# Differential attention on one core: the softmax bias is computed on VectorE instead of ScalarE

## The reference, cut to what matters

```python
def _diff_attend(q, k, v, lam):
    s = jnp.einsum('bhcqd,bhckd->bhcqk', q, k, preferred_element_type=jnp.float32) * (A_DQK ** -0.5)
    p = jax.nn.softmax(s, axis=-1)
    w = p[:, :, 0] - lam * p[:, :, 1]
    return jnp.einsum('bhqk,bhkd->bhqd', w.astype(v.dtype), v)
```

## Time and profile before

| | |
|---|---|
| three executions | 3625.79, 3628.02, 3628.82 us |
| profiled execution | 3625.79 us, span of the trace 3623.9 us |
| busy in the span | PE 3177.8 us (88%), DVE 1710.7 us (47%), ACT 1091.6 us (30%), POOL 301.6 us (8%) |
| costliest lines | PE L562 (the GEMM) 2133.4 + 1405.4 us; in attention PE L657 123.2 us, DVE L1454 194.7 us, ACT L1081 177.6 us |

### The profile page before, as it was taken

How to read it: one execution, slowest core, us unless ns; L and a number is a source line. 1 busy time by engine, 2 the same in 40 slices (tenths; PEclk the granted TensorE clock), 3 DMA queues, 4 the chain that set the end, 5 groups by cost and what they waited for, 6 DMA issues and landing times.

```text
span 3623.9 us, 44488 instructions
## 1 busy us (share of the span) xinstructions
PE 3177.8 (88%) x17262; PEld 1811.7 (50%) x17262; DVE 1710.7 (47%) x2202; ACT 1091.6 (30%) x1730; POOL 301.6 (8%) x208
## 2 busy tenths in 40 slices
PE   6799679778889999999999479679888899999997
PEld 6344554466444665555545234454665344444443
DVE  1794755676356210222225596655674463122235
ACT  2311213566344111111112411213664442111122
POOL 2400010000121000000002240010000210000001
PEclk8999769697999999999999699769898999999998
DMA  5110010111112321111112111011221232111113
GB/s 186 44 41 24 6 37 18 47 52 46 59 56 96 116 87 64 35 37 45 41 47 70 46 41 41 6 37 35 70 69 58 70 105 87 52 49 50 52 52 105
DMA packets 59449, 206.84 MB, mean 57 GB/s; under 512 B 7360, under 2 KB 8384, under 8 KB 59328
## 3 DMA queue, kind: packets, MB, share of 16 engines
q1 hardware_dynamic: 58176, 199.89, 16.5%
q10 hardware_dynamic: 1152, 5.24, 0.4%
HBM read 200.91 MB, written 4.19 MB: 57 GB/s over the span
## 4 chain that ended last, share of the span: by engine, by line
PE 55%; issue 24%; DVE 13%; ACT 5%; POOL 1%; DMA 1%; SPq 0%; POOLq 0%; DVEq 0%; ACTq 0%
PE PS L562 49%; DVE R L1597 4%; DVE wlo L1355 2%; ACT X L1050 1%; ACT R L1048 1%; PE PS L759 1%; DVE R L1433 1%; PE PS L620 1%; ACT whi L1003 1%; DVE R L1420 1%; POOL st L1960 1%; PE PS L815 1%; DVE R L1719 1%; DVE X L1693 0%; POOL X L1891 0%
## 5 line engine op out<-in xcount | busy, mean ns | idle before, releaser
L562 PE MATMUL PS<-R,whi 128*128 128x512 f16 (+1 forms) x7808 | 2133.4, 361 | 119.2 <-DVE wlo L1355 49.0
L562 PE MATMUL PS<-R,wlo 128*128 128x512 f16 (+1 forms) x3904 | 1405.4, 360 | 0.0
L562 PEld LDWEIGHTS PS<-R,whi 128*128 128x128 f16 x7808 | 766.3, 99 | 901.5 <-issue 70.6
L562 PEld LDWEIGHTS PS<-R,wlo 128*128 128x128 f16 x3904 | 385.3, 99 | 382.9 <-issue 19.3
L1355 DVE SCALAR_TENSOR_TENSOR wlo<-stage,whi 128x1024 f16<-128x1024 f32 (+1 forms) x260 | 332.0, 1277 | 512.0 <-ACT whi L1003 495.5
L1003 ACT ACTIVATE whi<-stage 128x1024 f16<-128x1024 f32 (+1 forms) x260 | 268.7, 1033 | 184.3 <-PE PS L562 135.0
L1891 POOL TENSOR_TENSOR X<-X 128x512 f32<-128x512 f32 (+2 forms) x105 | 154.4, 1473 | 1757.4 <-ACT X L1286 1613.6
L1454 DVE TENSOR_REDUCE tiny<-PS 128x1 f32<-128x1280 f32 (+1 forms) x144 | 194.7, 1370 | 96.1 <-PE PS L639 94.3
L1597 DVE SCALAR_TENSOR_TENSOR R<-X,small,R 128x1024 f32<-128x1024 f32 (+1 forms) x180 | 219.2, 1267 | 1.8
L1831 DVE SCALAR_TENSOR_TENSOR X<-X,PS 128x512 f32<-128x512 f32 (+3 forms) x60 | 62.0, 1033 | 303.2 <-PE PS L562 303.2
L1826 DVE SCALAR_TENSOR_TENSOR X<-X,PS 128x512 f32<-128x512 f32 (+3 forms) x60 | 62.1, 1035 | 297.2 <-ACT X L1303 297.2
(11 more groups left out here) (186 smaller groups left out, 2421.2 us busy)
## 6 DMA issues: line engine op xcount, KB each, us to landing
stage<-in_w_gu SPq DMA_DIRECT2D x120, 512.0 KB, 3.5
X<-in_w_ada SPq DMA_DIRECT2D x60, 512.0 KB, 3.4
stage<-in_w_down SPq DMA_DIRECT2D x48, 512.0 KB, 3.4
stage<-in_w_in SPq DMA_DIRECT2D x44, 512.0 KB, 3.4
stage<-in_w_out SPq DMA_DIRECT2D x32, 512.0 KB, 3.5
T<-in_w_ada SPq DMA_DIRECT2D x20, 512.0 KB, 3.5
R<-in_w_ada SPq DMA_DIRECT2D x16, 512.0 KB, 10.3
stage<-in_w_down SPq DMA_DIRECT2D x16, 384.0 KB, 3.0
```

Source lines behind the costliest of these rows:

```text
L562: last = mm(slot(j, t0, t1)[:, c0 - t0:c1 - t0], w[:, j, k, :], row, start=(k == 0 and q == 0), stop=(k == K - 1 and q == 2))
```

## The change

The bias is computed by VectorE, right behind each row maximum, by one `tensor_scalar` on 128x1 values, and ScalarE's two bias instructions go. The maximum is linked to the new instruction through `dve_own`. The semaphore between VectorE and ScalarE, `maxed`, becomes `nbias` and is raised by the new instruction. A new wait holds the new instruction until ScalarE has read the bias of two heads earlier from the same place. ScalarE's chain of own links in attention goes, VectorE's counts 8 more links per tile.

```diff
                 def exps(r, h, c):
                     n = 4 * r + h
-                    act.wait_ge(s("maxed"), 2 * n + (c + 1))
-                    if c:
-                        own.link(A(nbias[:, h % 2, c:c + 1], smax[:, h % 2, c:c + 1], ACT.Copy, scale=-SCORE))
-                    else:
-                        own.link(A(nbias[:, h % 2, c:c + 1], smax[:, h % 2, c:c + 1], ACT.Identity, scale=-SCORE,
-                                   bias=lamv[:, 12 + l:13 + l]))
+                    act.wait_ge(s("nbias"), 2 * n + (c + 1))
                     if not (isinstance(r, int) and n < 2):
 
                         act.wait_ge(s("w"), n - 1)
...
-                per = 2 * HA
                 tile(0, first=True)
                 with act.Fori(1, nt) as r:
-                    own.enter(r - 1, per)
                     tile(r)
-                own.leave(nt - 1, per)
...
                 def maxima(r, h, c):
                     n = 4 * r + h
                     dve.wait_ge(s("scores"), 2 * n + (c + 1))
-                    RED(smax[:, h % 2, c:c + 1], slot(c)[:, 0:keys], AX.X, ALU.max).then_inc(s("maxed"), 1)
+                    own.link(RED(smax[:, h % 2, c:c + 1], slot(c)[:, 0:keys], AX.X, ALU.max))
+                    if not (isinstance(r, int) and n < 2):
+                        dve.wait_ge(s("exps"), 2 * n + (c - 3))
+
+                    TS(nbias[:, h % 2, c:c + 1], smax[:, h % 2, c:c + 1], -SCORE, lamv[:, 12 + l:13 + l] if c == 0 else None,
+                       ALU.mult, ALU.add if c == 0 else ALU.bypass).then_inc(s("nbias"), 1)
...
-                per = 8 + 1 + 2
+                per = 8 + 8 + 1 + 2
```

More of the change, by code:

```diff
@@ L255, in build @@
             for run in (("c", "l") if l < LAYERS - 1 else ("l",)):
-                for n in "scores maxed exps w wt_ps wt pv pv_out".split():
+                for n in "scores nbias exps w wt_ps wt pv pv_out".split():
                     S[f"{n}_{run}{l}"] = sem(f"{n}_{run}_{l}")
```

## The result

The changed kernel took 3644.43 us in the median of 20 executions (3627.69 to 3684.58), the kernel before 3628.06 us beside it (3614.65 to 3637.36). The ratio is 1.0054, with a 95% interval of 1.0031 to 1.0077: slower by about half a per cent, where 0.26% less was forecast. The ratio leaves out the three slowest of them (over 3683 us, more than 1.5% above the fastest), the medians don't. The profiled execution took 3634.09 us, with a span of 3632.3 us; it is one of the quicker ones, so its profile shows less of the loss than the median has.

The account below looks back on a forecast made before the run. The prediction took a loop through several engines as the bound; 6.6 + 2.1 + 1.4 - 0.7 = 9.4 us saved gave 3618.6 us against the median, with 8 in 10 between 3609 and 3629 us.

Parts of the forecast that it names:

- The loop of a head, 0.33 us by the bias of map 0: Latent runs: map 0's exponential starts 0.33 us earlier in 20 heads, all passed on, 6.6 us gained.
- The loop of the context run: Context run: map 1's bias lies on the loop of 2.89 us; some 6 turns x 0.23 = 1.4 us gained.
- the 9.4 us of the sum: Whole kernel: total forecast saving, 6.6 + 2.1 + 1.4 - 0.7 us.
- Map 1's path to the exponential, +0.05 us: Heads 2 of 14 tiles: from maximum's end to exponential 0.05 us longer through VectorE, 0.7 us lost.
- `combine` 0.4 us later and hidden: Head 2: VectorE's extra work delays `combine` by 0.3 to 0.6 us, taken as 0.4, hidden by TensorE's wait for `out_lo`.
- the 0.15 us counted as gained in head 3: Head 3 of 14 tiles: 0.15 of map 0's 0.33 us reaches the modulation products, 2.1 us gained.
- its bad side: Latent runs: long stretches at 1.2 GHz become more; two more cost 12 us, 3631 us; chance 0.08.
- The price of a long stretch, 6.2 us: Latent tiles: one with 24 us at the lower clock takes 37.2 us where most take about 31.
- VectorE becomes the bound: Heads 2 and 3: `combine` late by more than 0.55 us delays TensorE; 14 us slower, 3642 us; chance 0.06.
- Optimizing Scalar/DVE Operations: VectorE against ScalarE: if VectorE is saturated, offloading to ScalarE may make sense; by it the change would be slower.

Follow-up runs that it names:

- map 1 alone: Against the kernel before, VectorE computes only the bias of map 1, ScalarE keeps that of map 0: ratio 1.0055, 3643.32 us.
- map 0 alone: Against the kernel before, VectorE computes only the bias of map 0, ScalarE keeps that of map 1: ratio 0.9948, 3605.76 us.
- The exchange: In head 2 VectorE takes map 1's maximum before `out_sum`: kernel before with it 0.9946, changed kernel with it 0.9969, both against the kernel before.
- the moved group: Layer 0's third group of modulation products moved from head 3 to head 2: before 1.0026, changed 0.9960, only map 0's bias on VectorE 0.9907.
- the added work: Layer 0's third group of modulation products computed also in head 2, first result overwritten: changed kernel 0.9973, only map 0's bias on VectorE 0.9894.
- ScalarE's two kept: Changed kernel, but ScalarE keeps its two bias instructions and writes results nobody reads: ratio 1.0086 to the kernel before, 3656.05 us.
- map 0 and the exchange: Only map 0's bias on VectorE, and map 1's maximum taken before `out_sum` in head 2: ratio 1.0005 to the kernel before, 3623.07 us.

## Why the prediction was wrong

Its own steps, in their order:

- *The loop of a head, 0.33 us by the bias of map 0: right.* 6.66 us a head at full clock, and the wait of 0.48 us shrank to 0.16. The loop of the context run is right as well (2.65 us). But this part alone (map 0) makes the kernel 0.52% faster, some 19 us, twice the 9.4 us of the sum, and the surplus is clock. In layer 1 of the changed kernel the quick tiles went from 30.3 to 28.3 us. Of that 0.32 and 0.40 us, in two heads, are the loop; 1.34 us goes with a stretch of 3.4 us at 1.2 GHz behind head 3. Each quick tile had one of at least that length before (transposes in 1.54 us instead of 0.88, values in 2.10 instead of 1.31); most tiles of layer 1 no longer have it.
- *Map 1's path to the exponential, +0.05 us: right* (+0.04).
- *`combine` 0.4 us later and hidden: mis-sized.* It was 0.6 us, the upper end of the range. TensorE's wait for it rose by 0.56 us, and of the 0.15 us counted as gained in head 3 about 0.06 us is left (from the scores of head 3 to the modulation products 2.78 us pass, before 2.84). By these terms alone the kernel would still be faster.
- *The step that failed: the clock had no term in the sum, and its bad side ("They could also come at other places and be more: two more long stretches cost 12 us") had a chance of 0.08.* The stretches at the lower clock are the largest term, with either sign. In the profiled execution layer 0's six tiles from 720.94 to 938.32 us took 36.2 us on average instead of 31.9; that is 26 us lost, while layer 1 gained 15.4 us. The loop was to save 9.4 us in all. In that run before, one stretch of 24 us stood among ones of 7 us or less; after, there are one of 37 us, two of 24, two of 14 and one of 10. In the median execution the balance is worse: 16 us slower, at a clock of 0.905.
- *The price of a long stretch, 6.2 us: too low.* It was taken against a tile that had a short stretch itself. A tile with 24 us at 1.2 GHz takes 37.7 us and one with 14 us 33.7 to 33.8, instead of 28.3 with none: about 0.4 us lost for each microsecond at that clock, 9.4 us for a long stretch.
- *The rival "VectorE becomes the bound": its place and its point (0.55 us) were passed, but its mechanism isn't what cost the time.* TensorE's longer wait costs little itself, as the quick tiles of layer 1 show, which have it too. The rule of the Trainium skill, "Perfetto Trace Analysis", section "Optimizing Scalar/DVE Operations", spoke against the change. It came out right in its sign for map 1 and not for map 0, and VectorE was not saturated in either. The rule of the Trainium skill, "VectorE: DVE Perf Modes", section "Rules for kernel authors", that the number of instructions counts and not the semaphores, agrees with the times of the two pairs with map 0, where leaving out the wait changed nothing. It does not with the changed kernel: a met wait with its register instruction was 0.09 us of gap each time, and without it the ratio was 0.9974 instead of 1.0054.

What is shown: the loss comes with map 1's part (map 1 alone, map 0 alone), and it goes with more time at the lower clock, in the profile and over all executions. TensorE's idle time in heads 2 and 3 of layer 0 is a cause of the low clock there. The exchange, the moved group and the added work each gave a higher clock in layer 0, in all eight profiles; the strongest evidence is the time of the two kernels with added work, which fell.

What isn't shown is how map 1's instruction brings the long stretches. The idle time of 2 us was there before the change. The later `combine` doesn't separate map 1 from map 0, nor layer 0 from layer 1. Theory D, that the loop's length beats with the clock, failed with ScalarE's two kept and with map 0 and the exchange, and was right for the other two kernels with the exchange, so it stays open. Nor is it shown why one tile has a stretch of 3 us and another one of 24 us after the same idle time. Layer 1 of the changed kernel ran at 0.98 and, with unchanged code and another start, at 0.74.

## What to carry to other kernels

Look at the granted clock by stage before adding up microseconds: where TensorE sits just below full use, stretches at the lower clock can cost more than the edit can save. Take several executions, since one profile gives a stage's clock only roughly. Of a change in two parts, try each part alone: here the one gave 0.5% and the other lost as much. A place where TensorE idles in every tile can be worth filling, even with work that is thrown away, but read the clock of every other stage again, since one of them may fall.

## What the runs showed of the hardware that was not expected

- Adding 16 matrix products (1.85 us) to each of layer 0's latent tiles made a kernel faster: a ratio of 0.9973 instead of 1.0054, and with map 0 alone 0.9894 instead of 0.9948.
- A busier TensorE can do less: in the same 180 us of layer 0 it was busy 153 us and did 991 products at a clock of 0.70, and busy 143 us with 1328 products at 1.00, with the same products in a tile.
- Stretches of 14 to 37 us at 1.2 GHz came in a run where no wait of TensorE was longer than 2.0 us. One profile showed 0.80, another 0.90 for the same stage in two kernels of the same time.
- A wait that is already met, with the register instruction for its value, put 0.09 us more between two linked instructions of VectorE (0.12 instead of 0.03 us).
- The new 128x1 instruction took 0.15 us without and 0.21 us with a pointer operand; ScalarE's took 0.20 and 0.29 us.
